# Twelve buffers for the first modulation chunks, five of sixteen chunks summed on TensorE, products of zeros and a new order in the first turn

## The reference

```
cond = silu(c)
mod = cond @ ada_w[l] + ada_b[l]            # 1024 x 9216 a layer
sh1, sc1, g1, sh2, sc2, g2, sh3, sc3, g3 = split(mod, 9)
hn = rms_norm(h, norm_g[l, 0]) * (1 + sc1) + sh1
h = h + 0.5 * g1 * ((silu(hn @ w_gate) * (hn @ w_up)) @ w_out)      # first feed-forward part
...                                           # mixing part, second feed-forward part
```

## Time and profile before

| | us |
|---|---|
| median of 3 executions | 2253.88 |
| lowest, highest of them | 2253.16, 2254.26 |
| profiled execution: span from first to last instruction (its only time on the page) | 2254.6 |
| TensorE busy | 2193.2 (97%) |
| VectorE busy | 1588.9 (70%) |
| ScalarE busy | 1097.0 (49%) |
| TensorE's share of the chain of waits that ended last | 90% |

### The profile page before, as it was taken

One profiled execution on the slowest core, in us unless ns is written; L12 is line 12 of the kernel. 1 busy time (PEld: TensorE's weight loads), 2 busy tenths in 40 slices (PEclk: granted clock), 3 DMA queues, 4 the chain that ended last, 5 costly groups with the idle time before them and its releaser, 6 DMA issues.

```text
span 2254.6 us, 31996 instructions
## 1 busy us (share of the span) xinstructions
PE 2193.2 (97%) x11883; PEld 1847.3 (82%) x11883; DVE 1588.9 (70%) x1904; ACT 1097.0 (49%) x1288; POOL 52.4 (2%) x94
## 2 busy tenths in 40 slices
PE   7999999999999998999999999999999999999998
PEld 6887886887788896888788799978878889998887
DVE  6787897885777798665655778665575567867555
ACT  4444574444543465444444465554454446565443
POOL 1000010000000010000000000000000000000000
PEclk9999999999999999999999999999999999999999
DMA  8996565985687565666555564455556655435663
GB/s 280 345 320 210 170 217 171 340 309 183 236 292 240 166 209 178 223 218 211 174 182 190 163 169 131 150 187 187 189 165 206 189 182 153 147 122 171 193 191 107
DMA packets 325042, 454.56 MB, mean 202 GB/s; under 512 B 32722, under 2 KB 270040, under 8 KB 324952
## 3 DMA queue, kind: packets, MB, share of 16 engines
q1 hardware_dynamic: 320952, 440.98, 59.7%
q0 software_dynamic: 3728, 11.31, 1.7%
q10 hardware_dynamic: 272, 1.05, 0.1%
HBM read 449.91 MB, written 1.05 MB: 200 GB/s over the span
## 4 chain that ended last, share of the span: by engine, by line
PE 90%; DVE 6%; ACT 2%; issue 1%; DMA 1%; SPq 0%; DVEq 0%; ACTq 0%
PE ps L626 21%; PE ps L628 21%; PE ps L627 20%; PE ps L619 5%; PE ps L620 5%; PE ps L621 5%; PE ps L797 2%; PE ps L779 1%; DVE wlo L1991 1%; PE ps L780 1%; PE ps L782 1%; PE ps L716 1%; PE ps L1072 1%; PE ps L745 1%; DMA arena<-in_ada_w_dram 1%
## 5 line engine op out<-in xcount | busy, mean ns | idle before, releaser
L1991 DVE TENSOR_TENSOR wlo<-raw,whi 128x2048 fp32r<-128x2048 f32 x348 | 791.4, 2278 | 354.7 <-ACT whi L1366 353.5
L1366 ACT ACTIVATE whi<-raw 128x2048 fp32r<-128x2048 f32 x346 | 660.2, 1910 | 274.4 <-PE ps L628 238.5
L626 PE MATMUL ps<-whi,xl 128*128 128x512 f32 x1472 | 591.7, 402 | 0.0
L628 PE MATMUL ps<-whi,xh 128*128 128x512 f32 x1472 | 574.2, 390 | 0.0
L627 PE MATMUL ps<-wlo,xh 128*128 128x512 f32 x1472 | 573.9, 390 | 0.0
L626 PEld LDWEIGHTS ps<-whi,xl 128*128 128x128 f32 x1472 | 276.5, 188 | 61.5 <-issue 4.7
L628 PEld LDWEIGHTS ps<-whi,xh 128*128 128x128 f32 x1472 | 276.4, 188 | 60.0
L627 PEld LDWEIGHTS ps<-wlo,xh 128*128 128x128 f32 x1472 | 276.8, 188 | 58.3 <-issue 4.3
L626 PE MATMUL ps<-whi,hidl 128*128 128x512 f32 x640 | 252.1, 394 | 1.4 <-DVE hidl L2183 1.4
L619 PE MATMUL ps<-xl,whi 128*128 128x256 f32 x864 | 249.3, 288 | 1.6 <-DVE wlo L1991 1.6
L628 PE MATMUL ps<-whi,hidh 128*128 128x512 f32 x640 | 249.2, 389 | 0.0
(11 more groups left out here) (405 smaller groups left out, 2342.8 us busy)
## 6 DMA issues: line engine op xcount, KB each, us to landing
raw<-in_ffn_w_in_dram SPq DMA_DIRECT2D x176, 512.0 KB
arena<-in_ada_w_dram SPq DMA_DIRECT2D x144, 512.0 KB, 6.2
raw<-in_w_in_dram SPq DMA_DIRECT2D x54, 1024.0 KB
raw<-in_ffn_w_out_dram SPq DMA_DIRECT2D x44, 1024.0 KB
raw<-in_w_ffn_gate_dram SPq DMA_DIRECT2D x88, 512.0 KB
raw<-in_w_ffn_up_dram SPq DMA_DIRECT2D x88, 512.0 KB
raw<-in_w_ffn_down_dram SPq DMA_DIRECT2D x44, 1024.0 KB
raw<-in_w_out_dram SPq DMA_DIRECT2D x16, 1024.0 KB
```

Source lines behind the costliest of these rows:

```text
L626: pe.matmul(o, al, wh, start=start, stop=False, **kw)
L628: return pe.matmul(o, ah, wh, start=False, stop=stop, **kw)
L1366: act.activation(whi[:, k % 3, :], raw[:, k % 3, :], ACT.Copy).then_inc(hi_done, 1)
L1991: tt(a[0], a[1], a[2].bitcast(F32), ALU.subtract).then_inc(lo_done, 1)
```

## The change

The ring `adaf` gets twelve buffers: the six old ones, and six in places that nobody needs yet (two more in `arena`, one in `side`, two in `gate`, one in `gain`). `ON_PE` becomes 2, 4, 5, 12, 14. The two new ones are worked by TensorE between the first and the second half of the first turn. Behind `mod_sums(0)` and `mod_sums(1)` TensorE issues eight and six products of zeros (bf16, 512 columns), whose results are overwritten. In the second half it works the eight products with `whi` first, waits for `wlo` only then, and works those with `wlo` apart. VectorE sums chunks 6 and 7 ahead of `lo` of unit 0, and chunks 8 and 9 behind `mod_columns(0)`.

The diff, cut to its core:

```diff
--- before.py
+++ after.py
@@ -170,7 +170,10 @@
         wsT = c1(8, P)
 
 
-        adaf = arena[:, 3072:9216].rearrange("p (i t n) -> p i t n", i=6, t=2)
+        adaf = [a.rearrange("p (t n) -> p t n", t=2) for a in
+                [arena[:, at:at + 1024] for at in (3072, 4096, 5120, 6144, 7168, 8192, 12800, ARENA - 1024)]
+                + [side[:, 0:1024], gate[:, 0, :], gate[:, 1, :], gain[:, :]]]
+        NADAF = len(adaf)
         accg = arena[:, 9216:10240]
         adag = arena[:, 5120:6144]
         T0 = 3072 + 2048 + 5632
@@ -211,7 +214,7 @@
         hi_done, lo_done, unit_used = sem("hi_done"), sem("lo_done"), sem("unit_used")
         x_loaded, c_loaded, out_stored = sem("x_loaded"), sem("c_loaded"), sem("out_stored")
         stage_loaded, smalls_loaded = sem("stage_loaded"), sem("smalls_loaded")
-        ada0_loaded = [sem(f"ada0_loaded{i}") for i in range(6)]
+        ada0_loaded = [sem(f"ada0_loaded{i}") for i in range(NADAF)]
         ada0_used = sem("ada0_used")
         adag_loaded, adag_used = sem("adag_loaded"), sem("adag_used")
         adam_loaded = [sem(f"adam_loaded{i}") for i in range(2)]
@@ -318,7 +321,7 @@
             else:
                 eng.wait_ge(acc_done, 3 * n + 2 * a + f + 1)
 
-        ON_PE = (2, 4, 5)
+        ON_PE = (2, 4, 5, 12, 14)
 
         def before0(i, pe):
             return sum((k in ON_PE) == pe for k in range(i))
@@ -413,9 +416,10 @@
 
             def ada_first(i):
 
-                if i >= 6:
-                    sp.wait_ge(*((ada0_summed, before0(i - 5, True)) if i - 6 in ON_PE else (ada0_used, before0(i - 5, False))))
-                sp.dma_start(adaf[:, i % 6], ada0[i % KC, :, i // KC, 0:2, :]).then_inc(ada0_loaded[i % 6], 16)
+                if i >= NADAF:
+                    j = i - NADAF
+                    sp.wait_ge(*((ada0_summed, before0(j + 1, True)) if j in ON_PE else (ada0_used, before0(j + 1, False))))
+                sp.dma_start(adaf[i % NADAF], ada0[i % KC, :, i // KC, 0:2, :]).then_inc(ada0_loaded[i % NADAF], 16)
 
             def first_unit(k):
 
@@ -643,11 +647,11 @@
             def mod_direct(i):
 
                 f, k = divmod(i, KC)
-                pe.wait_ge(ada0_loaded[i % 6], 16 * (i // 6 + 1))
+                pe.wait_ge(ada0_loaded[i % NADAF], 16 * (i // NADAF + 1))
                 for at in range(KC):
-                    w = adaf[:, i % 6, at // 4, P * (at % 4):P * (at % 4) + P]
+                    w = adaf[i % NADAF][:, at // 4, P * (at % 4):P * (at % 4) + P]
                     ins = pe.matmul(ps[:, 6 + f, at:at + 1], w, condT[:, 0, k:k + 1],
-                                    start=(at == 0 and i == 2), stop=False, skip_group_check=True)
+                                    start=(at == 0 and i in (2, 12)), stop=False, skip_group_check=True)
                 ins.then_inc(ada0_summed, 1)
 
             def turned0(kc):
@@ -668,24 +672,40 @@
 
                 pe.wait_ge(ada0_used, before0(KC * f + KC, False))
                 for at, col in mod_columns(f):
-                    ins = pe.matmul(ps[:, 6 + f, at:at + 1], acc[:, col:col + P], ones_col[:, 0:1], start=(f == 1 and at == 0),
+                    ins = pe.matmul(ps[:, 6 + f, at:at + 1], acc[:, col:col + P], ones_col[:, 0:1], start=False,
                                     stop=True, skip_group_check=True)
                 ins.then_inc(mod_summed, 2)
+
+            def zero_products(k, bank=0):
+
+                for _ in range(k):
+                    pe.matmul(ps[:, bank, :], zerow[:, :], zerow[:, 0:1].to_broadcast([P, 512]), start=True, stop=True,
+                              skip_group_check=True)
 
             def first_turn(L):
 
                 pe.wait_ge(minus_ready, 1)
                 for f in range(2):
                     mod_sums(f)
-                    split_ready(L, f)
+                    zero_products(8 if f == 0 else 6, 0 if f == 0 else 6)
                     wh, wl = as4(whi, f), as4(wlo, f)
+                    if f == 0:
+                        split_ready(L, 0)
+                    else:
+                        pe.wait_ge(hi_done, L.unit(1) + 1)
                     for hh in range(2):
                         pe.wait_ge(xh_ready, 2 * f + hh + 1)
                         for a in range(2):
                             for q in (2 * hh, 2 * hh + 1):
                                 kc, tok = 4 * f + q, slice(a * P, a * P + P)
-                                pe.matmul(ps[:, a, :], xh[:, kc, tok], wl[:, q, :], start=(kc == 0), stop=False)
+                                if f == 0:
+                                    pe.matmul(ps[:, a, :], xh[:, kc, tok], wl[:, q, :], start=(kc == 0), stop=False)
                                 pe.matmul(ps[:, a, :], xh[:, kc, tok], wh[:, q, :], start=False, stop=False)
+                    if f == 1:
+                        split_ready(L, 1)
+                        for a in range(2):
+                            for q in range(4):
+                                pe.matmul(ps[:, a, :], xh[:, 4 + q, a * P:a * P + P], wl[:, q, :], start=False, stop=False)
                     pe.wait_ge(x_ready, 2 * f + 2)
                     for a in range(2):
                         for q in range(4):
@@ -694,6 +714,9 @@
                         if f == 1 and a == 0:
                             ins.then_inc(gu_ready, 1)
                     ins.then_inc(unit_used, 1)
+                    if f == 0:
+                        mod_direct(12)
+                        mod_direct(14)
 
             def turn_setup(part):
 
@@ -727,12 +750,6 @@
                     pe.wait_ge(gate0_read, 2 * e + q)
                 pe.matmul(ps[:, MB, :], ones_row[:, :], accg[:, 512 * q:512 * q + 512], start=True,
                           stop=True).then_inc(gate0_summed, 1)
-
-            def zero_products(k):
-
-                for _ in range(k):
-                    pe.matmul(ps[:, 0, :], zerow[:, :], zerow[:, 0:1].to_broadcast([P, 512]), start=True, stop=True,
-                              skip_group_check=True)
 
             def turn_x(n, a, f):
 
@@ -1882,13 +1899,13 @@
             def ada_first(i):
 
                 f, k = divmod(i, KC)
-                dve.wait_ge(ada0_loaded[i % 6], 16 * (i // 6 + 1))
+                dve.wait_ge(ada0_loaded[i % NADAF], 16 * (i // NADAF + 1))
                 o = acc[:, 0:2048].rearrange("p (j n) -> p j n", j=2)[:, :, 512 * f:512 * f + 512]
                 if i in (0, KC):
-                    ts(o, adaf[:, i % 6], condT[:, 0, k:k + 1], None, ALU.mult).then_inc(ada0_used, 1)
+                    ts(o, adaf[i % NADAF], condT[:, 0, k:k + 1], None, ALU.mult).then_inc(ada0_used, 1)
                     return
                 dve.wait_ge(ada0_used, before0(i, False))
-                stt(o, adaf[:, i % 6], condT[:, 0, k:k + 1], o, ALU.mult, ALU.add).then_inc(ada0_used, 1)
+                stt(o, adaf[i % NADAF], condT[:, 0, k:k + 1], o, ALU.mult, ALU.add).then_inc(ada0_used, 1)
 
             def first_roots():
 
@@ -2121,16 +2138,16 @@
             def first():
 
                 L = layers()[0]
+                ada_first(6)
+                ada_first(7)
                 lo(L, 0)
-                for i in range(6, KC + 2):
-                    ada_first(i)
                 mod_columns(0)
-                for i in range(KC + 2, KC + 5):
-                    ada_first(i)
+                ada_first(8)
+                ada_first(9)
                 rest_first(0, 0)
-                ada_first(KC + 5)
+                ada_first(10)
                 rest_first(0, 1)
-                for i in (KC + 6, KC + 7):
+                for i in (11, 13, 15):
                     ada_first(i)
                 mod_columns(1)
                 dve.drain().then_inc(adam_used, 2)
```

## The result

| | us |
|---|---|
| before, 7 executions beside the change | median 2253.88, 2252.14 to 2256.49 |
| changed, 7 executions | median 2260.92, 2257.55 to 2262.29 |
| ratio | 1.0027, 95% interval 1.0017 to 1.0036 |
| profiled execution of the change: time and span | 2260.92 and 2259.1 |

The change makes the kernel slower, by 0.27% or 6.1 us by the ratio; the two medians differ by 7.0. The forecast was +3.2 us, with "same" as the likeliest outcome (0.76) and "slower", over 2258.4, at 0.22: by that bound it came out slower. The median lies 0.9 us above the forecast range, the ratio times the median of before (2260.0) on its upper end.

The account below looks back on a forecast made before the run. The prediction held TensorE, busy 97% of the span, to bound the kernel, leaving only the opening's waits and clock. Terms -1.4 + 3.7 + 0.9 = +3.2 us gave 2253.88 + 3.2 = 2257.1 us, range 2254.9 to 2260.0.

Parts of the forecast that it names:

- Buffers at 0 us: Twelve chunk buffers: weight unit 1 lands 3.7 us earlier, but its split still waits behind the modulation read; worth 0 us.
- rival (4): Loads bound the opening after all and unit 1's 3.7 us come through: 2250.2 us, chance 0.03.
- VectorE's order hidden: Chunks 6 and 7 ahead of unit 0's split finish before 25, needed at 28.50; VectorE is done by 37.91 as before.
- Zeros ahead, -1.4 us: Eight zero products before the first half raise the clock sooner; first half ends at 37.9 instead of 39.30.
- Direct sums, +3.7 us: Chunks 12 and 14 on TensorE behind the first half: 32 one-column passes at 0.115 us, all on the way to T1.
- the clock in them, +0.9: Clock falls at 42.5, 4.6 us after the last dense product; the remaining 0.9 us of one-column work takes 1.8.
- T1: End of the second group of modulation sums: 41.14 us in the old trace, forecast 44.3.
- T1 carries over to the restart through SyncE's chain: Split of unit 1, unit 4, 23 small loads, unit 5, chunk, `hidl`: a later T1 moves the restart by as much.
- the restart: TensorE resuming after its wait for `hidl`, at 65.13 us in the old trace.
- rival (3): Delay is absorbed behind T1, as the load queue empties while SyncE is late: 2254 to 2255.5 us, chance 0.08.
- The restart goes from 65.13 to 68.3; TensorE arrives 1.9 later and stands still for about 2.7 us instead of 1.4: TensorE's wait for `hidl` behind the first turn: the +3.2 us at T1 passes to the restart and the total time.
- the clock falls early in the direct sums: Most one-column passes run at 0.222 us; T1 at 45.9 to 46.6, +4.8 to +5.5 us, chance 0.21.

Follow-up runs that it names:

- b_buffers: Kernel before with only the twelve chunk buffers; ratio to before 1.0003.
- a_dve_sums: The change with chunks 12 and 14 given back from TensorE to VectorE, all else kept; ratio to before 1.0020, +4.5 us.
- after_again: The changed kernel, unaltered, timed and profiled once more; ratio to before 1.0028.
- a_no_zeros: The change without its eight and six products of zeros; ratio to before 1.0029, +6.5 us.
- a_chunks89: The change with chunks 12 and 14 back on VectorE and chunks 8 and 9 ahead of the first modulation read; ratio to before 1.0022.
- a_hold: The change with a product of zeros behind every second direct sum of chunks 12 and 14, eight in all; ratio to before 1.0031, +7.0 us.
- b_setup_early: Kernel before with the 23 small loads issued ahead of the load of unit 4; ratio to before 0.9995.
- b_direct: Kernel before with only chunks 12 and 14 moved to TensorE; ratio to before 1.0026, +5.9 us.
- a_setup_early: The change with the 23 small loads issued ahead of the load of unit 4; ratio to before 1.0006, +1.4 us.
- best: The change with chunks 12 and 14 on VectorE, chunks 8 and 9 ahead of the first modulation read, and small loads ahead of unit 4; ratio to before 0.9999.

## Why the forecast was right, and where it was wrong

*Buffers at 0 us*: right, shown by b_buffers, and rival (4) falls with it. *VectorE's order hidden*: right in that VectorE was done at 36.3, long before it was asked; a_dve_sums shows that this holds only while two chunks are off VectorE. *Zeros ahead, -1.4 us*: right in this pair, with luck. From the end of the first sums to that of the first half it was 9.41 us, forecast 37.9 - 28.5 = 9.4, before 10.97. But the kernel before had a late rise of the clock in this profile: over all profiles this stretch took 9.4 to 11.0 us in six without zeros and 8.5 to 9.8 in eight with them, 1.0 us less on the mean. *Direct sums, +3.7 us, and the clock in them, +0.9*: right. The forecast had 6.4 us from the end of the first half to T1; the three profiles of this program gave 5.3, 5.7 and 7.9, mean 6.3. The rule of the Trainium skill (TensorE: Matmul & The Clock Gate, section LDWEIGHTS), a load of 107 ns with no word on the clock, does not hold here at the lower level: 16 passes took 3.55 us where the granted clock was 0.50 and 1.84 to 1.93 where it was 1.00. *T1 carries over to the restart through SyncE's chain*: right, and the strongest result: the restart kept its distance of about 24 us from T1 in ten profiles (rival (3), that the delay is absorbed, falls), and with the small loads out of that chain the distance is 21 us and 4.7 of 6.1 us are gone.

The step that fell short is "The restart goes from 65.13 to 68.3; TensorE arrives 1.9 later and stands still for about 2.7 us instead of 1.4", taken as the end of the sum. The standstill was 3.44 and 2.43 us in the two profiles, on either side of the forecast, and T1 from the first direct sum was 31.8, 29.3 and 34.8 us in the three profiles of this opening against 29.7, 29.5, 28.5 and 28.5 in four with the old one: +2.9 us on the mean, near the +3.2 forecast. Counted from the end of the first sums, which leaves the early end in after_again out, it is +3.7. What was left out is the lower clock further on, behind the restart and in two later places. In the first profile it fell in the standstill, and 1.35 us went into the products behind the restart; in a_no_zeros and a_chunks89 it was low from 69.9 and from 64.3 us, and no profile without a wait for `hidl` has a low stretch there. Second, 1295 and 1875 us: +1.4 and +0.9 us in the first profile, and both stretches again in the second. Of the six profiles of kernels made from the change with a wait for `hidl`, four show both, a_dve_sums the later one and a_hold none; of the eight others one (b_setup_early) shows the later one. The program is the same there. That the opening decides this is an inference from these counts: no run moved a late stop by itself, and it stays open. So in the change's own traces the later T1 is shown to reach the restart, but half of the difference between the spans (2.3 of 4.5 us, and 2.4 of 2.8 in the second pair) lies in stretches whose cause is open. Of the kernels that cost about 6 us, only b_direct has its whole difference ahead of the restart. In the pair of first profiles the sum is 1.32 (restart) + 1.35 + 1.4 + 0.9 - 0.7 = 4.3 of the 4.5 us between the spans. The ratio gives 1.6 us more than that (6.1), which fits the old kernel's profile being of a slow execution and the 1.1 us by which the changed one began earlier, but no trace shows it.

The chance of 0.76 for "same" rested on those missing terms, and on a measurement that tells 0.2%: the interval came out at 0.1% to either side, enough to tell even 3.2 us. The prediction also set the page's span (2254.6) beside the timed median as if both were one measure; the sum does not hang on it. The rival "the clock falls early in the direct sums" gave 4.8 to 5.5 us, near the size measured, and b_direct and a_setup_early show such falls (at 40.9 and 40.1 us, inside the direct sums); but in the first profile of the change the clock held through the direct sums, and the loss came later. So the range held the ratio by a hair, for a reason partly other than the one for which it was made wide.

## What to carry to other kernels

Before moving work to an engine that looks free, ask who stands behind its last instruction: in b_direct 3.7 us planned on TensorE cost 6, because the clock fell in them and the split of the next unit, and behind it one load queue with 23 small loads, waited for the same sums. Taking the work back is no cure by itself, if the other engine is then the last (a_dve_sums, +4.5 us). Small loads that nobody needs soon belong ahead of a wait in the issuing engine's program, not behind it. And price a longer stop of TensorE with the lower clock that may follow it: 1.35 us behind the restart here.

## What was not expected of the hardware

- Dense products of zeros stood between the one-column passes in a_hold, and the clock stayed at 1.00 from 28.8 to 62 us in its one profile; without them it fell at 42.0, 39.3 and 40.1 in the three profiles of this opening.
- The same kind of stop lets the clock fall or not. The wait for `hidl` was followed by 0.50 in the change (3.44 us, low from 65.9), in a_chunks89 (3.31) and in a_no_zeros (1.91), and not in after_again (2.43), a_dve_sums (2.52) and a_hold (2.79). After the shorter waits of before, b_buffers and b_direct (1.17 to 1.51) it was not. So the length of the wait alone does not tell a fall here, and a forecast can only give such a stop a chance of one.
- The time from the first direct sum to the end of the first sums, the same work in all kernels here, was 17.1 us in most profiles and 14.7 in four of them (after_again, a_hold, best, a_chunks89), where the 32 passes of chunks 4 and 5, right behind the transposes of the input, took 3.8 to 4.0 us instead of 6.8, so mostly at the upper level. All four are kernels made from the change; the five others made from it and the five with the old opening took 17.1. In the four the clock rose at 16.5 to 18.8 us, in the transposes or less than 1 us behind them, and was down again by 22.3. What decides it was not tested.
